# The linear recurrence moved among the dilated attention's projections, in a two-block transformer kernel

## What is computed

```
z = h @ w_in;  lru_x, lru_gate, q, k, v = split(z)      # 512, 512, 768, 768, 768 columns
xc = causal_dwconv(lru_x) + conv_b
r, i = sigmoid(xc @ wa + ba), sigmoid(xc @ wx + bx)     # block-diagonal
a = exp(-8 * r * softplus(-lam));  bt = sqrt(1 - a^2) * i * xc
hs[t] = a[t] * hs[t-1] + bt[t]                          # the recurrence
y_lru = hs * gelu(lru_gate)
y_att = for each of 4 heads: 3 groups (dilation 1, 4, 16) of causal attention
        on rmsnorm(q) * Dh^-0.5, rmsnorm(k), merged by their log-sum-exp
out = concat(y_lru, y_att) @ w_out
```

## Time and profile before

| | us |
|---|---|
| median of three executions | 2069.72 |
| lowest, highest | 2067.46, 2076.98 |
| the profiled execution | 2072.59 |
| its span, first to last instruction | 2070.7 |
| mean granted TensorE clock | 0.982 of full |
| PE busy | 1979.7 (96%) |
| DVE busy | 1525.1 (74%) |
| ACT busy | 1104.7 (53%) |
| POOL busy | 111.7 (5%) |

### The profile page before, as it was taken

How to read it: one execution, slowest core, us unless ns; L and a number is a source line. 1 busy time by engine, 2 the same in 40 slices (tenths; PEclk the granted TensorE clock), 3 DMA queues, 4 the chain that set the end, 5 groups by cost and what they waited for, 6 DMA issues and landing times. The chain is left out here.

```text
span 2070.7 us, 38196 instructions
## 1 busy us (share of the span) xinstructions
PE 1979.7 (96%) x14497; PEld 1836.8 (89%) x14497; DVE 1525.1 (74%) x2351; ACT 1104.7 (53%) x1777; POOL 111.7 (5%) x76
## 2 busy tenths in 40 slices
PE   7999998999999999999889999998989999989999
PEld 7999988889999999989788899998989998879998
DVE  6777876657777776778666777776988888677887
ACT  5445654554544555457435644544745555575554
POOL 0000011010000000000210100000600000000000
PEclk9999999999999999999999999998999999999999
DMA  5555542343555555545323345555445554514654
GB/s 208 185 185 193 161 149 83 103 132 134 171 184 182 193 164 187 185 160 186 114 71 133 130 155 172 183 182 167 134 139 163 187 187 154 183 68 141 198 183 142
DMA packets 90966, 327.82 MB, mean 158 GB/s; under 512 B 10224, under 2 KB 11376, under 8 KB 90736
## 3 DMA queue, kind: packets, MB, share of 16 engines
q1 hardware_dynamic: 90288, 324.24, 47.5%
q10 hardware_dynamic: 576, 2.16, 0.3%
HBM read 325.31 MB, written 1.05 MB: 158 GB/s over the span
## 5 line engine op out<-in xcount | busy, mean ns | idle before, releaser
L2001 PE MATMUL ps<-a_both,w_hi 128*128 128x256 f32 (+1 forms) x7104 | 1621.5, 316 | 22.5 <-DVE a_both L1168 7.6
L2001 PEld LDWEIGHTS ps<-a_both,w_hi 128*128 128x128 f32 x7104 | 1173.8, 192 | 117.6 <-DVE w_lo L1126 9.5
L2001 PE MATMUL ps<-a_both,w_lo 128*128 128x256 f32 x4464 | 1260.9, 283 | 0.0
L1126 DVE TENSOR_TENSOR w_lo<-raw,w_hi 128x1024 fp32r<-128x1024 f32 x614 | 750.8, 1228 | 279.5 <-ACT w_hi L505 279.1
L2001 PEld LDWEIGHTS ps<-a_both,w_lo 128*128 128x128 f32 x4464 | 855.1, 192 | 0.0
L505 ACT ACTIVATE w_hi<-raw 128x1024 fp32r<-128x1024 f32 x614 | 634.1, 1049 | 129.6 <-DMA raw<-stream 72.3
L1042 POOL TENSOR_TENSOR sc<-sc,nhalf 128x2 f32<-128x2 f32 (+5 forms) x25 | 61.4, 2457 | 1684.6 <-DVE sc L1152 1260.8
L2001 PE MATMUL ps<-w_hi,a_both 128*128 128x512 f32 (+2 forms) x464 | 140.2, 380 | 6.7 <-DVE a_both L1202 4.4
L1194 DVE TENSOR_TENSOR arena<-ps,arena 128x512 f32<-128x512 f32 x114 | 78.8, 691 | 66.5 <-ACT arena L567 66.1
L562 ACT ACTIVATE arena<-arena 128x256 f32<-128x256 f32 x88 | 36.8, 418 | 170.4 <-DVE arena L1226 144.0
L573 ACT ACTIVATE a_both<-arena 128x256 fp32r<-128x256 f32 x132 | 55.2, 418 | 134.3 <-DVE arena L1234 104.2
(11 more groups left out here) (322 smaller groups left out, 1335.5 us busy)
## 6 DMA issues: line engine op xcount, KB each, us to landing
raw<-stream SPq DMA_DIRECT2D x613, 512.0 KB, 3.3
gates<-late ACTq DMA_DIRECT2D x1, 1088.0 KB, 6.7
out<-x SPq DMA_DIRECT2D x8, 128.0 KB, 2.0
con<-consts SPq DMA_DIRECT2D x1, 544.0 KB, 8.6
raw<-stream ACTq DMA_DIRECT2D x1, 512.0 KB, 3.9
x<-x_in ACTq DMA_DIRECT2D x2, 256.0 KB, 5.6
x<-x_in SPq DMA_DIRECT2D x2, 256.0 KB, 5.3
par<-params SPq DMA_DIRECT2D x1, 451.0 KB, 6.7
```

The costliest lines, as they stand in the source:

```text
L1126: V.tensor_tensor(w_lo[:, u % SLOTS, :], raw[:, u % RAW, :], w_hi[:, u % SLOTS, :], ALU.subtract).then_inc(split_ready, 1)
L2001: return nc.tensor.matmul(o, a, b, start=start, stop=stop, **k)
```

## The change

On TensorE the gate products `r` and `i` move from behind units 8 to 11 to behind units 0 to 3, into banks 2, 3 and 0, 1; units 8 to 11 now wait for "ith". On ScalarE the gate tanhs follow `gth`; exp and tanh of the recurrence follow the splits 4 and 5 (that is, of units 9 and 10); the square root follows `squares("k")`, ahead of `split(8)`; the rounded copy of the output follows `squares("q")`, ahead of the copies of q and k. On VectorE "xin" follows `split(4)`, "m2" `split(5)`; the two products follow `variances("k")`; the scans and L1953 follow `split(9)`, ahead of the scaling of k; L1956 stands directly ahead of `dmax(0)`. No instruction is added or dropped but one extra wait, and all shapes stay.

```diff
--- before.py
+++ after.py
@@ -234,9 +234,9 @@
 
 
 PE2_STEPS = ["cfps", "mean", "lnstat", "lnbc", "dgT", "r", "i", "qT", "kT"]
-DVE2_STEPS = ["cf0", "cf1", "cen0", "cen1", "ysc_lo0", "lnvar", "lndiag", "ysc_lo1", "yb0", "yb1", "o2_0", "o2_1", "o2_lo0", "o2_lo1", "lamz", "dg", "xc", "dgcol", "sp4", "gin", "dvark", "dk", "dvarq", "xin",
-              "m2", "ylru", "ylru_lo"]
-ACT2_STEPS = ["diag0", "diag1", "diag2", "diag3", "lnsq0", "lnsq1", "ysc_hi0", "ysc_hi1", "lnth0", "lnth1", "o2_hi0", "o2_hi1", "spe", "lgsq", "gth", "ksq", "rth", "qsq", "ith", "qT", "kT", "a", "tq", "mult", "ylru_hi"]
+DVE2_STEPS = ["cf0", "cf1", "cen0", "cen1", "ysc_lo0", "lnvar", "lndiag", "ysc_lo1", "yb0", "yb1", "o2_0", "o2_1", "o2_lo0", "o2_lo1", "lamz", "dg", "xc", "dgcol", "sp4", "gin", "xin",
+              "m2", "dvark", "ylru", "dk", "dvarq", "ylru_lo"]
+ACT2_STEPS = ["diag0", "diag1", "diag2", "diag3", "lnsq0", "lnsq1", "ysc_hi0", "ysc_hi1", "lnth0", "lnth1", "o2_hi0", "o2_hi1", "spe", "lgsq", "gth", "rth", "ith", "a", "tq", "ksq", "mult", "qsq", "ylru_hi", "qT", "kT"]
 POOL2_STEPS = ["lnrs", "drsk", "drsq"]
 
 
@@ -934,29 +934,18 @@
                 dil_evac(0)
                 act.wait_ge(*DV2.at(0, "gin"))
                 nc.scalar.activation(gin, gin, ACT.Tanh, scale=0.7978845608028654).then_inc(*AC2.sig(0, "gth"))
-                dil_split(4, 5, 6, 7)
-                dil_evac(1)
-                squares("k", 2)
-                dil_split(8, 9, 10, 11)
-                dil_evac(2)
                 act.wait_ge(*PE2.at(0, "r"))
                 for i in range(4):
-                    q = nc.scalar.activation(thr[:, i, :], bank(6 + i // 2, (i % 2) * TOK, (i % 2 + 1) * TOK), ACT.Tanh,
+                    q = nc.scalar.activation(thr[:, i, :], bank(2 + i // 2, (i % 2) * TOK, (i % 2 + 1) * TOK), ACT.Tanh,
                                              scale=0.5, bias=half("lru_ba", i))
                 q.then_inc(*AC2.sig(0, "rth"))
-                squares("q", 3)
                 act.wait_ge(*PE2.at(0, "i"))
                 for i in range(4):
-                    q = nc.scalar.activation(thi[:, i, :], bank(4 + i // 2, (i % 2) * TOK, (i % 2 + 1) * TOK), ACT.Tanh,
+                    q = nc.scalar.activation(thi[:, i, :], bank(0 + i // 2, (i % 2) * TOK, (i % 2 + 1) * TOK), ACT.Tanh,
                                              scale=0.5, bias=half("lru_bx", i))
                 q.then_inc(*AC2.sig(0, "ith"))
-                act.wait_ge(*PE2.at(0, "qT"))
-                act.wait_ge(*DV2.at(0, "dk"))
-                nc.scalar.activation(flat(qTd), ps[:, 0:3, :], ACT.Copy).then_inc(*AC2.sig(0, "qT"))
-                act.wait_ge(*PE2.at(0, "kT"))
-                act.wait_ge(*DV2.at(0, "xin"))
-                nc.scalar.activation(flat(kTd), ps[:, 3:6, :], ACT.Copy, scale=dgain).then_inc(*AC2.sig(0, "kT"))
-                dil_split(12)
+                dil_split(4, 5)
+                act.wait_ge(*AC2.at(0, "rth"))
                 act.wait_ge(*DV2.at(0, "sp4"))
                 for i in range(4):
                     k = sc[:, 296 + i:297 + i]
@@ -966,6 +955,23 @@
                     k = sc[:, 296 + i:297 + i]
                     q = nc.scalar.activation(tqb[:, i, :], thr[:, i, :], ACT.Tanh, scale=k, bias=k)
                 q.then_inc(*AC2.sig(0, "tq"))
+                dil_split(6, 7)
+                dil_evac(1)
+                squares("k", 2)
+                act.wait_ge(*DV2.at(0, "m2"))
+                nc.scalar.activation(thr, thr, ACT.Sqrt).then_inc(*AC2.sig(0, "mult"))
+                dil_split(8, 9, 10, 11)
+                dil_evac(2)
+                squares("q", 3)
+                act.wait_ge(*DV2.at(0, "ylru"))
+                nc.scalar.activation(a_hi[:, 8:12, :], thi, ACT.Copy).then_inc(*AC2.sig(0, "ylru_hi"))
+                act.wait_ge(*PE2.at(0, "qT"))
+                act.wait_ge(*DV2.at(0, "dk"))
+                nc.scalar.activation(flat(qTd), ps[:, 0:3, :], ACT.Copy).then_inc(*AC2.sig(0, "qT"))
+                act.wait_ge(*PE2.at(0, "kT"))
+                act.wait_ge(*DV2.at(0, "xin"))
+                nc.scalar.activation(flat(kTd), ps[:, 3:6, :], ACT.Copy, scale=dgain).then_inc(*AC2.sig(0, "kT"))
+                dil_split(12)
                 dil_split(13)
 
                 def d_exps(h):
@@ -986,8 +992,6 @@
                 dil_split(15)
                 dil_evac(3)
                 d_turned(0)
-                act.wait_ge(*DV2.at(0, "m2"))
-                nc.scalar.activation(thr, thr, ACT.Sqrt).then_inc(*AC2.sig(0, "mult"))
                 dil_split(16)
                 d_turned(1)
                 dil_split(17)
@@ -997,8 +1001,6 @@
                 d_high(0)
                 d_turned(2)
                 d_turned(3)
-                act.wait_ge(*DV2.at(0, "ylru"))
-                nc.scalar.activation(a_hi[:, 8:12, :], thi, ACT.Copy).then_inc(*AC2.sig(0, "ylru_hi"))
                 d_high(1)
                 for k in range(6):
                     split(POS["od_out"] + k + AHEAD)
@@ -1873,11 +1875,20 @@
                 dve.wait_ge(*AC2.at(0, "lgsq"))
                 link(V.tensor_scalar(flat(gin), flat(gin), 0.044715, 1.0, ALU.mult, ALU.add))
                 V.tensor_tensor(flat(gin), flat(gin), flat(lg), ALU.mult).then_inc(*DV2.sig(0, "gin"))
-                for i in range(2, 8):
+                for i in range(2, 4):
                     split(d0 + i + AHEAD)
                 dve.wait_ge(*AC2.at(0, "gth"))
                 tick(V.scalar_tensor_tensor(flat(gin), flat(gin), 1.0, flat(lg), ALU.add, ALU.mult))
-                split(d0 + 8 + AHEAD)
+                split(d0 + 4 + AHEAD)
+                dve.wait_ge(*AC2.at(0, "ith"))
+                V.scalar_tensor_tensor(flat(thi), flat(thi), 1.0, flat(xc), ALU.add, ALU.mult).then_inc(*DV2.sig(0, "xin"))
+                split(d0 + 5 + AHEAD)
+                dve.wait_ge(*AC2.at(0, "tq"))
+                link(V.tensor_tensor(flat(thr), flat(aa), flat(aa), ALU.mult))
+                link(V.scalar_tensor_tensor(flat(tqb), flat(thr), 1.0, flat(tqb), ALU.add, ALU.mult))
+                V.tensor_scalar(flat(thr), flat(tqb), -1.0, 2.0 ** -100, ALU.mult, ALU.max).then_inc(*DV2.sig(0, "m2"))
+                for i in range(6, 9):
+                    split(d0 + i + AHEAD)
 
                 def variances(i):
                     dve.wait_ge(*AC2.at(0, i + "sq"))
@@ -1885,7 +1896,16 @@
                     V.tensor_scalar(dss[i], dss[i], 1.0 / DD, EPS, ALU.mult, ALU.add).then_inc(*DV2.sig(0, f"dvar{i}"))
 
                 variances("k")
-                for i in range(9, 12):
+                dve.wait_ge(*AC2.at(0, "mult"))
+                link(V.scalar_tensor_tensor(flat(tqb), flat(tqb), -2.0 ** -100, flat(thr), ALU.is_le, ALU.mult))
+                dve.wait_ge(*DV2.at(0, "xin"))
+                link(V.scalar_tensor_tensor(flat(thi), flat(thi), 0.5, flat(tqb), ALU.mult, ALU.mult))
+                split(d0 + 9 + AHEAD)
+                for i in range(4):
+                    e = tick(V.tensor_tensor_scan(tqb[:, i, :], aa[:, i, :], thi[:, i, :], 0.0, ALU.mult, ALU.add))
+                need(e)
+                V.scalar_tensor_tensor(flat(thi), flat(gin), 0.5, flat(tqb), ALU.mult, ALU.mult).then_inc(*DV2.sig(0, "ylru"))
+                for i in range(10, 12):
                     split(d0 + i + AHEAD)
                 dve.wait_ge(*PO2.at(0, "drsk"))
                 for j in range(TT):
@@ -1893,12 +1913,12 @@
                     e = V.tensor_tensor(r, r, over(drs["k"][:, 12 * j:12 * j + 12], DD), ALU.mult)
                 e.then_inc(*DV2.sig(0, "dk"))
                 variances("q")
-                dve.wait_ge(*AC2.at(0, "ith"))
-                V.scalar_tensor_tensor(flat(thi), flat(thi), 1.0, flat(xc), ALU.add, ALU.mult).then_inc(*DV2.sig(0, "xin"))
                 split(d0 + 12 + AHEAD)
                 rq = drs["q"]
                 dve.wait_ge(*PO2.at(0, "drsq"))
                 link(V.tensor_scalar(rq, rq, DD ** -0.5, None, ALU.mult))
+                dve.wait_ge(*AC2.at(0, "ylru_hi"))
+                V.tensor_tensor(a_lo[:, 8:12, :], thi, a_hi[:, 8:12, :], ALU.subtract).then_inc(*DV2.sig(0, "ylru_lo"))
 
                 def dmax(h):
 
@@ -1930,30 +1950,16 @@
                 dmax(1)
                 dnorm(0)
 
-                dve.wait_ge(*AC2.at(0, "tq"))
-                link(V.tensor_tensor(flat(thr), flat(aa), flat(aa), ALU.mult))
-                link(V.scalar_tensor_tensor(flat(tqb), flat(thr), 1.0, flat(tqb), ALU.add, ALU.mult))
-                V.tensor_scalar(flat(thr), flat(tqb), -1.0, 2.0 ** -100, ALU.mult, ALU.max).then_inc(*DV2.sig(0, "m2"))
                 split(d0 + 14 + AHEAD)
                 dnorm(1)
                 split(d0 + 15 + AHEAD)
-                dve.wait_ge(*AC2.at(0, "mult"))
-                link(V.scalar_tensor_tensor(flat(tqb), flat(tqb), -2.0 ** -100, flat(thr), ALU.is_le, ALU.mult))
-                dve.wait_ge(*DV2.at(0, "xin"))
```

(18 more changed lines are left out.)

## The result

The changed kernel takes 2081.49 us (median of 20 executions, 2070.66 to 2085.41) against 2074.11 for the kernel before (median of 20). The ratio is 1.0031, with a 95% interval of 1.0019 to 1.0043: by it the changed kernel is 6.4 us slower, 3.9 to 8.9. The forecast was 5.7.

The account below looks back on a forecast made before the run. TensorE, busy 96%, bounds the kernel. Late k (+6.4) becomes +8.3 at dmax(0), less 1.3 for a table load; up to od_out +4.3 to +7.0 by clock, middle +5.7: 2069.7 + 5.7 = 2075.4 us, range 2068 to 2082.

Parts of the forecast that it names:

- k is late by 6.4: TensorE's transposes of k: they wait for VectorE's scaling of k, ready at 1818.2 instead of 1808.25; +6.4 us.
- The loads of the weights, 0: Weights five units ahead: later low halves on VectorE and the loads they release still come in time; cost 0.
- q and `dmax(0)`, +8.3: Start of softmax: q's variances, GpSimd's power, rq and the output's low half put dmax(0) at 1826.6, not 1818.29; +8.3 us.
- the 1.9 to spare: Ahead of dmax(0): the scores, there at 1824.7, would be ready 1.9 us before dmax(0) starts.
- Unit 16 to `turn(3)`, -1.3: Softmax: the second table load, directly ahead of d_exps(2), goes away and shortens the way to turn(3) by 1.30 us.
- The clock: Up to od_out: +7.0 with the recorded fall, +4.3 if the clock holds, middle +5.7; fall ahead of unit 16 taken as 0.
- DVE keeps up: Rival: VectorE's idle time takes the moved work, k is ready when q is transposed; -2.4 us, 2067.3 us; chance 0.10.
- Near nothing: Rival: k late, but VectorE faster there or waits ahead of turn(2), turn(3) shrink; within 2 us of before; chance 0.08.
- GpSimd blocks DVE: Rival: GpSimd's power for k and VectorE's two-operand work wait for each other; k 5.07 us later, 2080.5; chance 0.03.
- The clock falls more than once: Rival: clock falls ahead of unit 16 and of turn(3), with the other bounds; +10 to +12 us, 2080 to 2082; chance 0.12.
- The drain: Beside each ScalarE table load: by the skill's rule some 1.38 us more, lowering the forecast by 1.4; prediction left it out.
- the load ahead of `d_exps(0)`: Table load moved ahead of d_exps(0) on ScalarE, which waits there for dmax(0): bounded 0 to 1.28 us, taken as 0.

Follow-up runs that it names:

- e1: Changed kernel with scans and their product behind q's variances, output's high half behind split(13), low half ahead of dmax(2); ratio to the kernel before 1.0003.
- e2: e1 with VectorE's variances of k also ahead of split(8); ratio to the kernel before 0.9996.
- e3: Changed kernel with the four scans done twice; not timed, region 96.75 us in its profile.
- e4: Kernel before with only TensorE's early gate products and ScalarE's two early tanhs of the change; ratio to the kernel before 1.0005.
- e5: Kernel before with a one-column exponential ahead of dil_evac(4), bringing the table load into ScalarE's idle time; ratio to the kernel before 0.9974.
- e10: e5 run again, unchanged; ratio to the kernel before 0.9983.
- e7: The changed kernel run again, unchanged; ratio to the kernel before 1.0031.
- e6: e2 with dil_evac(3) ahead of split(15) on ScalarE; ratio to the kernel before 0.9982.
- e8: e6 with TensorE's unit 12 ahead of the transposes of q; ratio to the kernel before 0.9995.
- e9: Kernel before with the one-column exponential ahead of dil_evac(4) and dil_evac(3) ahead of split(15); ratio to the kernel before 0.9987.

## Why the prediction was right, and where it was off

**k is late by 6.4.** Worked out: square root done and the high half of unit 13 ready at 1803.9, k scaled at 1818.2. Measured, less 6.06: 1804.0 and 1818.4; k's transposes +6.66. e1, e2 and e3 show that VectorE's queue is what sets it, with a slope of one.

**The loads of the weights, 0.** This term had a cost that stayed hidden. The load of unit 16 waits until VectorE has done the low half of unit 13, here at 1811.3; ScalarE's high half of unit 16 then waited 2.57 for it (row 1814.61), and with it the copy of units 8 to 11, which were done at 1815.0. q's transposes waited 1.64 instead of the 1.1 worked out (1.11 in e4). The 0.5 lies under the wait for k.

**q and `dmax(0)`, +8.3.** Measured +9.2. The step that failed is which came last: not `rq`, but the scores, for which VectorE waited 1.15 (row 1833.58). They were late by the half clock behind the long wait: from the start of k's transposes to that of the scores, the transposes and unit 12, it is 6.76 us instead of 4.17. That is 2.6, the 1.9 to spare is used up, and 0.9 comes on top with the 0.2 by which k itself was later than worked out. I had bounded this by 0 to 0.8 and taken 0. GpSimd's power took 4.16, not 5.07, but that didn't decide it: with 5.07 VectorE would have been ready for `dmax(0)` some 0.6 ahead of the scores still.

**Unit 16 to `turn(3)`, -1.3.** Less the half clock it is -1.4 (20.35 before; 20.43 less 1.5). At whole clock that has two reasons of which I had named one: by e5 the table load alone gives 0.7 of it. That VectorE's softmax steps were held by the recurrence ahead of `dmax(2)` I had passed over ("beside PE's wait, not in it"). So the nearness of this term is in part luck: with the clock half at unit 16, as it was, the table load alone gives all of it (e10).

**The clock.** I had left the recorded fall behind `turn(3)` half in (+4.3 or +7.0, taken 5.7) and set a second fall ahead of unit 16 at 0. It was the other way round: from unit 16 to `turn(1)` it is 4.47 in the changed kernel instead of 2.97, +1.5, and behind `turn(3)` 4.58 instead of 7.41, -2.8. The sum: 9.2 + 1.5 - 1.4 - 2.8 = 6.5. In e7, the same kernel again, the way behind `turn(3)` took 6.21, and the sum is 8.0. That the total came so near is in part luck: two errors upwards, 0.9 at `dmax(0)` and 1.5 at unit 16, were mostly made up for by one of 1.5 downwards behind `turn(3)`, where I had taken the middle, 6.05.

**The rivals.** "DVE keeps up" is refuted by the 14.4 us without idle time. e2, in which k is nearly in time, has its `dmax(0)` 1.34 later than before, where this rival said 1.6, but that doesn't bear out its arithmetic: in e2 q's variances start 1.4 later than the rival has them, the power is 0.6 shorter, and the low half of 1.2 doesn't stand ahead of `dmax(0)`. "Near nothing", within 2 us of before, is outside the interval of 3.9 to 8.9. "GpSimd blocks DVE" is refuted too: beside the power for k (1813.24 to 1818.31) stand the second product, a low half and most of the scans, at 1.22, 1.23 and 2.43 us, as elsewhere; it was not VectorE that waited. The contention that the Trainium skill states for VectorE instructions with two SBUF inputs (SBUF — State Buffer, Who interferes with whom) does show in this case, in GpSimd's own durations and off the critical path (last section). "The clock falls more than once" was half true, at a price of 2.4 and with a fall less elsewhere.

**The drain** of 1.38 us that the Trainium skill states beside a table load (ScalarE: Activation LUTs, What ACT_TABLE_LOAD costs) isn't seen. The square root starts 0.02 behind the end of its table load here too (1806.72 + 1.28 to 1808.02), and the load ahead of `d_exps(0)` ran inside ScalarE's wait (1832.48, then 3.27 of wait): my 0 for it was right. In e5, where a load left the way, the exponentials came 1.4 earlier and not 2.7.

## What to carry to other kernels

Work moved from where an engine is on the critical path to where it is idle a third of the time (3.4 of 10 us) is free only if nothing behind it in that engine's queue is due soon: count the engine's instructions from the last thing it waits for to the next thing that somebody waits for (here 14.3 us), not its busy share. Then order the queue by who waits: the steps with a long way behind them (the variances, GpSimd's power, the scaling) first, those that nobody needs for long (the scans, which in e2 start at 42 for an `od_out` at 85) into the waits behind. A gain on the way in one engine, such as a table load, is cut off where the next engine's queue becomes last, so look at both before counting it.

## What was not expected of the hardware

GpSimd's power on the same 128x24 tile took 5.07, 4.47 or 4.16 us, and which it was repeated from one execution to another. The first two rows are of the changed kernel, the third is of e1:

```profile
1813.24 5.07 POOL L1044 TENSOR_TENSOR sc<-sc,nhalf 128x24 f32<-128x24 f32 x1 [63.93 <-DVE sc L1896]
1826.37 4.16 POOL L1044 TENSOR_TENSOR sc<-sc,nhalf 128x24 f32<-128x24 f32 x1 [8.06 <-DVE sc L1896]
...
1821.67 4.47 POOL L1044 TENSOR_TENSOR sc<-sc,nhalf 128x24 f32<-128x24 f32 x1 [4.46 <-DVE sc L1896]
```

It goes with what VectorE is doing at the moment when the power starts. In all twelve traces (24 such powers):

| VectorE at the start of the power | us | which |
|---|---|---|
| nothing | 4.16, 4.17 | q in the changed kernel, e3, e7; k in e2, e6, e8 |
| a scan with 0.52 us left | 4.47, 4.48 | q in e1, e2, e6, e8 |
| a 128x1024 instruction with two SBUF inputs, 1.05 us left | 5.07, 5.08 | k and q in before, e4, e5, e9, e10; k in the changed kernel, e1, e3, e7 |

So beside the changed kernel's first row stands L1900 (1813.07, 1.22 us) in VectorE's rows, and beside its second nothing (VectorE is idle from 1826.30 to 1829.85). The smaller powers elsewhere in the kernel before do the same: on 128x2 they take 0.70 with VectorE idle, 1.61 with a weight's low half running (two SBUF inputs, 1.05 us left), and 0.71 beside an instruction that has one of its inputs in PSUM, with 0.53 left. The power thus seems to wait for the rest of that one instruction, and the two-input instructions that start during it cost neither engine anything here (1.22 and 1.23 us as elsewhere). No experiment set this apart, but no power in the traces departs from it. It had no price in the time, since neither power was the last to come in the changed kernel.

The same stalls did not always bring the clock down. e5 and e10 are the same kernel. Ahead of unit 16 the wait is 2.23 us in both, behind nine transposes, yet unit 16 and what follows it up to `turn(1)` ran at whole clock in the one and mostly at half in the other, 2.96 or 4.45 us; with the changed order the clock fell there in all three executions looked at (it, e3, e7). Behind `turn(3)` the way to `od_out` took 7.41 and 7.12 us in the two kernels with a wait of 2.43 ahead of `turn(2)` (before, e4). In the ten with a wait of 1.0 to 1.55 there it took 6.14 to 6.22 in eight, and 4.58 in two (the changed kernel's first execution, and e1). So one profile of a kernel with such waits carries some 1.5 us of chance at unit 16 (e5 against e10) and 1.6 behind `turn(3)` (the changed kernel against e7); the other 1.2 behind `turn(3)` goes with the shorter wait.
